# 128 unused bytes ahead of the kernel's upper SBUF tensors are taken out

## The reference

```
proj  = x @ w_in[l]                      # q, k, v | a, gate
attn  = causal attention of 8 heads of 64 with rotary q and k
conv  = swish(LayerNorm(depthwise conv, width 31, of a * sigmoid(gate)))
x     = LayerNorm(alpha * x + concat(attn, conv) @ w_out[l])
q     = x @ w_q                          # 8 heads x 2 halves of 128
s     = q . sub_keys; top 16 of each half, then top 16 of the pair sums
gates = softmax(best scores)
h     = gelu(x . u_tab[e]) for each chosen expert e of 16384
x     = LayerNorm(alpha * x + sum over e of gates * h * v_tab[e])
```

## Time and profile before

| what | value |
|---|---|
| median of 3 runs | 1886.78 us (1886.64 to 1886.89) |
| the profiled execution: time, span | 1886.89 us, 1885.0 us |
| TensorE matmul (PE) busy | 1868.9 us, 99% of the span |
| weight loads (PEld) busy | 1608.3 us, 85% |
| VectorE (DVE) busy | 1460.2 us, 77% |
| ScalarE (ACT) busy | 955.1 us, 51% |
| GpSimd (POOL) busy | 356.1 us, 19% |
| DMA | 333.06 MB, mean 177 GB/s |
| granted TensorE clock | 1.00 of full speed |

### The profile page before, as it was taken

The page is one execution under the profiler, slowest core; times in us unless marked ns, Lnnn a source line. Parts: engine busy times, 40 slices in busy tenths (PEclk is TensorE's granted clock), DMA queues, the critical chain, the costliest instruction groups (busy, mean ns, idle before and its releaser), DMA issues.

```text
span 1885.0 us, 38932 instructions
## 1 busy us (share of the span) xinstructions
PE 1868.9 (99%) x13240; PEld 1608.3 (85%) x13240; DVE 1460.2 (77%) x2548; ACT 955.1 (51%) x1553; POOL 356.1 (19%) x269
## 2 busy tenths in 40 slices
PE   8999999999999999999999999999999999999998
PEld 7789998888888888888887899988888888888886
DVE  7869998788888888544498699977888888884445
ACT  4655456555554444454546554555555544444454
POOL 0000000000004444455400000000000044444543
PEclk9999999999999999999999999999999999999999
DMA  7444555545444454766564455555454454547553
GB/s 251 145 162 157 179 194 197 176 157 168 165 167 162 161 174 160 246 194 194 168 211 135 158 170 181 196 197 168 158 168 166 156 176 160 173 161 250 192 191 122
DMA packets 95964, 333.06 MB, mean 177 GB/s; under 512 B 11680, under 2 KB 16032, under 8 KB 95648
## 3 DMA queue, kind: packets, MB, share of 16 engines
q1 hardware_dynamic: 88992, 317.51, 51.0%
q10 hardware_dynamic: 6912, 14.77, 2.5%
HBM read 328.20 MB, written 4.03 MB: 176 GB/s over the span
## 4 chain that ended last, share of the span: by engine, by line
PE 93%; DVE 3%; DMA 2%; issue 1%; ACT 1%; ACTq 0%; POOL 0%; DVEq 0%; SPq 0%; POOLq 0%
PE bank L1589 20%; PE bank L1362 14%; PE bank L1364 14%; PE bank L1363 14%; PE bank L1588 9%; PE bank L1608 5%; PE bank L1327 4%; PE bank L1329 4%; PE bank L1328 4%; PE bank L1591 1%; PE bank L1431 1%; DMA shifted_u<-x_kept 1%; DVE top_index_u L1043 1%; PE bank L1556 1%; DMA x_kept<-u_pad 0%
## 5 line engine op out<-in xcount | busy, mean ns | idle before, releaser
L779 DVE TENSOR_TENSOR lo<-raw,hi 128x1024 fp32r<-128x1024 f32 x600 | 757.0, 1263 | 225.7 <-ACT hi L453 224.4
L453 ACT ACTIVATE hi<-raw 128x1024 fp32r<-128x1024 f32 x600 | 633.1, 1057 | 452.7 <-PE bank L1364 407.7
L431 POOL TENSOR_TENSOR w_split<-h,w_split 128x256 fp32r<-128x256 f32 x256 | 353.9, 1383 | 1513.2 <-ACT w_split L712 1128.4
L1589 PE MATMUL bank<-xt,hi 128*128 128x512 f32 x1600 | 559.6, 397 | 0.0
L1362 PE MATMUL bank<-hi,w_split 128*128 128x512 f32 x1024 | 405.2, 396 | 0.9 <-POOL w_split L431 0.9
L1364 PE MATMUL bank<-hi,w_split 128*128 128x512 f32 x1024 | 399.4, 390 | 0.0
L1363 PE MATMUL bank<-lo,w_split 128*128 128x512 f32 x1024 | 398.3, 389 | 0.0
L1588 PE MATMUL bank<-xt,lo 128*128 128x256 f32 x1400 | 390.0, 279 | 0.0
L1589 PEld LDWEIGHTS bank<-xt,hi 128*128 128x128 f32 x1600 | 290.7, 188 | 52.3
L1588 PEld LDWEIGHTS bank<-xt,lo 128*128 128x128 f32 x1400 | 263.6, 188 | 8.9
L1364 PEld LDWEIGHTS bank<-hi,w_split 128*128 128x128 f32 x1024 | 192.1, 188 | 41.4
(11 more groups left out here) (190 smaller groups left out, 1751.7 us busy)
## 6 DMA issues: line engine op xcount, KB each, us to landing
raw<-in_stream SPq DMA_DIRECT2D x600, 512.0 KB, 3.4
shifted_u<-x_kept ACTq DMA_DIRECT2D x16, 142.0 KB, 4.6
ln_g<-in_ln_p ACTq DMA_DIRECT2D x4, 512.0 KB, 7.8
ln_b<-in_ln_p ACTq DMA_DIRECT2D x4, 512.0 KB, 9.5
keys_sb<-in_keys_t ACTq DMA_DIRECT2D x2, 1024.0 KB, 4.9
x_kept<-x ACTq DMA_DIRECT2D x4, 512.0 KB, 4.6
x<-x_kept ACTq DMA_DIRECT2D x4, 512.0 KB, 7.1
shifted_u<-x_kept ACTq DMA_DIRECT2D x8, 130.0 KB, 4.4
```

The source lines that it names most:

```text
L431: nc.gpsimd.tensor_tensor(ws[:, j, 1, :], h[:, ds(i * (RING * SEQ) + j * SEQ, SEQ)], ws[:, j, 0, :].bitcast(f32), ALU.subtract).then_inc(* ...
L453: nc.scalar.activation(hi[:, j, :], raw[:, j, :], ACT.Copy).then_inc(*hi_done.one)
L779: vec.tensor_tensor(lo[:, j, :], raw[:, j, :], hi[:, j, :].bitcast(f32), ALU.subtract).then_inc(*lo_done[j].one)
L1589: last = mm(dst[:, :], w_hi, both, start=k == 0, stop=k == KC - 1)
```

## The change

One line goes: the 128 bytes between `gate_part` and `xt`. Everything placed behind it, `xt`, `w_split`, `ones`, `ident_b`, `causal`, `small`, `h` and all that lies inside `h`, starts 128 bytes lower. `raw`, `hi`, `lo`, `x` and what shares its space, `ident`, `iota`, `key_blocks` and `gate_part` stay where they are, and so does everything in PSUM and DRAM. No instruction is added, removed or moved.

```diff
         key_block = place("key_blocks", [P, 5, SEG], bf16)
         gate_part = place("gate_part", [P, GROUPS, PARTS, GROUP, 2], bf16)
 
-        used[0] += 128
         xt_at = used[0]
         xt = place("xt", [P, KC, 2, SEQ], f32r)
         ws = place("w_split", [P, RING, 2, SEQ], f32r, at=xt_at)
```

## The result

The changed kernel takes 1905.27 us at the median of 4 runs (1904.85 to 1908.27), the kernel before 1886.84 us beside it: a ratio of 1.0101 over all their runs, 95% interval 1.0089 to 1.0113 (the quotient of the two medians is 1.0098). By the medians it is slower by 18.4 us. The range of the prediction ended at 1893.

What follows compares the result with a forecast made beforehand. The prediction took TensorE's matmul pace to bound the kernel, busy 1868.9 of 1885.0 us. Its terms summed as 1886.89 + 0 + 0 + 0 + 0, giving 1886.8 us from the median of 1886.78, range 1880 to 1893 us.

Steps and rivals of the forecast that it cites:

- what the prediction says of the second half of the V stage: Second half of V stage: DVE, ACT and POOL each busy about half of 178 us.
- Moved operands of DVE, ACT and POOL: Instructions of these engines on moved tensors: 0; the copies into w_split could cost 4.4 us of ACT's time, hidden.
- the 1% that was said: Sign in the profile after: groups of DVE, ACT and POOL stay within 1% each.
- DMAs: Transfers into and out of h: 0, with bounds of -2.1 to +2.1 us from the two waits for shifted_u.
- TensorE, the step that failed: Matmuls whose weights and moving operand change distance: taken as 0, bounds 0 and +17.5 us.
- The first rival: Whole V stage takes mixed's slower pace, 5.7 ns more for each matmul with w_split: 1904.3 us, chance 0.12.
- the alternating wide tiles: Wide U stage: tiles take 2.77, 2.82 and 2.78 us, every other one losing about 0.04 us.
- The test on the convolution's matmuls: Line 1431: 288 matmuls with stepped operand addresses last 376 to 404 ns, median 379; in steady state they do not differ.
- the 288 cycles for 256 columns: Wide U tiles: 32 cycles over the columns for each matmul, so a tile would take 2.773 us.
- Both rivals on them: Wide U tiles all take the longer length, +4.0 us, chance 0.08, or the shorter, -4.0 us, faster case 0.10.
- the row: Output projection: matmuls with mixed as weights start every 232.2 against 226.5 ns on the same lines; up to +17.5 us.

Runs made afterwards that it cites:

- The pattern probe: Changed kernel plus narrow, wide and V tiles on TensorE alone at its end, 16 operand offsets; wide tiles at distance 0 took 2808, 2788 and 2816 ns.

## Why the prediction was wrong

*What bounds the kernel.* Right: PE's pace and little else, before and after. What the prediction says of the second half of the V stage is right too; its window is not among:

```profile
755.00:933.00 178.00, 178.00 (x826) 147.40 (x823) 84.64 (x70) 89.71 (x132) 88.72 (x66) 1.00 0.63 207
```

*Moved operands of DVE, ACT and POOL.* Right at 0. Copies into w_split take 401 ns after 400; line 590's copies into mixed took 417 ns both times, with source and target both on and then both 128 past a multiple of 256. With source and target of the w_split copies both on (w_split alone raised) they take 402 ns, with both past (w_split alone put back) 400. So the 17 ns between the two groups is not an alignment. One group moved by more than the 1% that was said: DVE's onehots<-key_blocks,i_t, from 998 to 1013 ns, and its operands did not move.

*DMAs.* Right within the bounds: waits for shifted_u 2.5 us from 2.1.

*TensorE, the step that failed.* The prediction took this term as 0 out of bounds of 0 and +17.5 us. It measured 15.4 us in V by the copies' starts and 15.6 us by putting w_split back, with 2.9 us in U beside it. The first rival had the place right, the cause in that the distance of the two operands sets the pace, and the price nearly: 5.7 ns were read from mixed, and V lost 6.5 and 5.6 ns for a matmul in the second half of the two layers but 4.2 ns in the first half, with gate matrices, 5.1 over all. That its 1904.3 us came so near to 1905.27 is in part luck: 2 us too much for V and nothing for U. It was given a chance of 0.12 for two reasons, and both were errors of reading:

- "A slow pace also shows where the addresses are the same as those of a fast neighbour", of the alternating wide tiles. The pattern probe shows uneven tiles at one fixed distance with all other engines idle, and even ones at distance 16; in the kernel too the alternation went with xt at 128, 16 and (up to the transposes) 144. So it is itself an effect of the distance, and no witness against addresses.
- "Modulo 512 the distances differ from mixed's of today." They do, and the distances of 128 and 384 turned out equally slow. The trace before could not tell the two periods apart, so by my estimate this should have halved the chance at most.

Two more readings failed beside them. The test on the convolution's matmuls took durations for the pace, and it was of another kind of matmul: plain float32 with 32 columns of weights, of which four start close together every 216 ns in the rows of line 1431. That nothing varies there says nothing of fp32r with 128 columns. And the 288 cycles for 256 columns were taken as the pace without loss, but alone they start every 113.3 ns at distances 64 and 88, which is 272 cycles at 2.4 GHz. By that both lengths of the wide tile lie over an estimated 8 x (226.7 + 113.3) ns = 2.72 us, though no run here had wide tiles under 2.77 for long.

What spoke for the rival was the stronger sort of evidence: the same three lines of code, without waits, at two paces that each held for 5 us or more with the operands' place as the difference.

*The wide tiles.* Both rivals on them missed: neither length won, all tiles took their mean. The loss in U, 2.9 us, is in the pairs with gate matrices, for which there was no term. The prediction also had no term for xt as weights, the 1.1 to 1.4 us of the input projections.

The prediction had set a rule of the Trainium skill against the row, from "SBUF — State Buffer", "Who interferes with whom": PE never waits on anyone for SBUF. As far as other engines go the runs don't contradict it, for the slow pace is the same with them idle (232.4 ns) as in V (233.2 and 232.3). The error was to let it speak for TensorE's own two operands. In "TensorE: Matmul & The Clock Gate", "Step-by-step: what each phase is for" under Part 2, the Trainium skill adds that loading the next weights doesn't take read bandwidth from the running matmul. With TensorE alone at work the 512-column pace moved between 226.7 and 234.3 ns with nothing but the weights' place, so here the two reads do disturb each other, or something does that depends on both addresses in the same way; the runs show the dependence, not the circuit.

## What to carry to other kernels

Where TensorE is the bound and float32 weights are loaded for each matmul, the distance in SBUF between weights and moving operand is a parameter worth up to 3% for 512 columns and 6 to 8% for 256 with TensorE alone; in this kernel 128 bytes cost 1.0%, and the best distances tried gave 0.2%. The spare bytes of a layout are not always free to remove. Measure it with a stretch of matmuls at the kernel's end that has every other engine idle, in the true order of a tile, and then try the best distance in place, for what the matmuls ahead leave behind also counts. When the same line shows two steady paces without waits, and only the operands' place differs, take the place for the likelier cause until a run says otherwise, and count every matmul that reads a moved tensor, as weights too.

## What the runs showed of the hardware that was not expected

- TensorE's pace in fp32r depends on the distance modulo 256 bytes between weights and moving rows. In plain rows of matmuls with all other engines idle it was 226.7 ns at 0 and 120, up to 234.3 at 96, for 512 columns; 113.3 ns at 64 and 88, up to about 122 at 24, for 256. Steps of 8 bytes already change it.
- The distance does not settle it. At 16 a V tile's matmuls took 227 ns and plain rows 233.3; narrow tiles at 16 took 2.72 and 2.84 us in one stage; the V stage at 128 took 168.37 or 167.68 us for the same tiles.
- It does so in rhythms that repeat: for 512 columns at distance 128 every seven matmuls with mixed, in the second layer's V stage and with all other engines idle, but every two in the first layer's V stage.
- 128 bytes more ahead of h, from which TensorE reads in the later U and the V stage for six transposes of a layer alone, cost 2.3 us in each layer's U tiles with gate matrices. That a rhythm outlasts what started it is the likely reading, not shown apart from ACT's and DVE's use of h.
